# Conformer convolution layer: the token axis cut in two halves, norm and output projection of the first half placed beside the convolution of the second, output bias added early

## The reference, cut to what matters

```
x = x + conformer_conv(rms_norm(x, norm1_g[0]), ...)
x = x + hierarchical_moe(rms_norm(x, norm2_g[0]), ...)

def conformer_conv(h, w_in, b_in, dw, dw_b, ln_g, ln_b, w_out, b_out):
    u = h @ w_in + b_in
    a, g = jnp.split(u, 2, axis=-1)
    u = a * jax.nn.sigmoid(g)
    u = causal_depthwise_conv(u, dw, width=31) + dw_b     # per channel, over 31 tokens
    u = jax.nn.silu(layer_norm(u, ln_g, ln_b))            # mean and variance over the 1024 channels
    return u @ w_out + b_out
```

## Time and profile before

| what | value |
|---|---|
| median of three runs | 1702.82 us |
| the profiled execution | 1700.86 us, of which 1699.1 us are the span from the first to the last instruction |
| mean granted PE clock | 0.926 |
| busy: PE, DVE, ACT, POOL | 1408.8, 440.7, 328.0, 277.2 us |
| 16 DMA engines, mean rate | 278 GB/s |

### The profile page before, as it was taken

The page is one execution under the profiler, slowest core; times in us unless marked ns, Lnnn a source line. Parts: engine busy times, 40 slices in busy tenths (PEclk is TensorE's granted clock), DMA queues, the critical chain, the costliest instruction groups (busy, mean ns, idle before and its releaser), DMA issues.

```text
span 1699.1 us, 17050 instructions
## 1 busy us (share of the span) xinstructions
PE 1408.8 (83%) x6028; PEld 638.2 (38%) x6028; DVE 440.7 (26%) x858; ACT 328.0 (19%) x629; POOL 277.2 (16%) x381
## 2 busy tenths in 40 slices
PE   4996596898878788777599999996997888888784
PEld 2442144333223223232376676644332332233231
DVE  1699615111011111010333333325110110110112
ACT  2465311000000000000334434421010000000000
POOL 0688200211111111110000000000211111111110
PEclk9998697999999999898799999997998999999997
DMA  9122015789999999998600400315899999999994
GB/s 324 37 99 99 1 74 222 318 361 419 420 420 420 420 421 418 419 416 339 248 1 1 149 1 1 149 74 223 338 360 420 421 420 420 420 416 413 418 413 184
DMA packets 91249, 473.13 MB, mean 278 GB/s; under 512 B 19675, under 2 KB 19675, under 8 KB 40260
## 3 DMA queue, kind: packets, MB, share of 16 engines
q1 hardware_dynamic: 78500, 443.12, 64.3%
q0 software_dynamic: 10400, 16.82, 2.7%
q10 hardware_dynamic: 2304, 12.58, 1.9%
HBM read 466.43 MB, written 23.33 MB: 288 GB/s over the span
## 4 chain that ended last, share of the span: by engine, by line
PE 49%; DMA 33%; DVE 7%; POOL 4%; issue 3%; SPq 3%; ACT 1%; ACTq 0%; POOLq 0%; DVEq 0%
DMA ring<-in_moe_w 30%; PE banks L1273 19%; PE banks L1381 7%; PE banks L1221 5%; POOL scratch L515 4%; PE banks L1290 3%; PE banks L1414 3%; SPq L315 2%; PE banks L1170 2%; DVE banks L863 2%; PE banks L1473 1%; PE banks L1428 1%; PE banks L1455 1%; DMA area<-y_dram 1%; PE banks L1402 1%
## 5 line engine op out<-in xcount | busy, mean ns | idle before, releaser
L1273 PE MATMUL banks<-ring,scratch 128*64 128x512 f32 x1984 | 502.2, 657 | 143.8 <-DMA ring<-in_moe_w 131.3
L1273 PEld LDWEIGHTS banks<-ring,scratch 128*64 128x64 f32 x1984 | 157.9, 151 | 484.8 <-issue 484.8
L1006 DVE COPY scratch<-banks 128x256 f32<-128x256 f32 x65 | 27.6, 424 | 801.7 <-PE banks L1281 801.7
L1290 PE MATMUL banks<-ring,scratch 128*64 128x512 f32 x1008 | 231.8, 602 | 3.0 <-DVE scratch L1006 3.0
L680 ACT ACTIVATE scratch<-banks 64x512 f32<-64x512 f32 x65 | 38.2, 588 | 598.8 <-PE banks L1273 598.8
L533 POOL COPY at_out<-rows_out 128x1 int32 (+1 forms) x64 | 11.6, 181 | 705.2 <-ACT scratch L684 705.2
L515 POOL TENSOR_TENSOR scratch<-scratch 128x512 f32<-128x512 f32 x88 | 111.8, 1271 | 63.6 <-ACT scratch L652 51.6
L1381 PE MATMUL banks<-hT,ring 128*128 128x512 f32 x256 | 117.9, 604 | 0.8 <-DVE hT L820 0.8
L1170 PE MATMUL banks<-hT,ring 128*128 128x512 f32 x256 | 113.2, 603 | 0.7 <-issue 0.7
L1290 PEld LDWEIGHTS banks<-ring,scratch 128*64 128x64 f32 x1008 | 68.3, 137 | 118.7 <-issue 111.7
L1221 PE MATMUL banks<-ring,area 128*128 128x512 f32 x200 | 91.3, 609 | 10.6 <-ACT area L662 9.6
(11 more groups left out here) (205 smaller groups left out, 1144.6 us busy)
## 6 DMA issues: line engine op xcount, KB each, us to landing
ring<-in_moe_w SPq DMA_DIRECT2D x374, 1024.0 KB, 16.9
area<-in_moe_w SPq DMA_DIRECT2D x12, 1024.0 KB, 10.2
ring<-in_attn_w_qkv SPq DMA_DIRECT2D x12, 1024.0 KB, 14.6
ring<-in_conv_w_in SPq DMA_DIRECT2D x8, 1024.0 KB, 14.4
area<-y_dram ACTq DMA_DIRECT2D x8, 1024.0 KB, 7.9
ring<-in_conv_w_out SPq DMA_DIRECT2D x4, 1024.0 KB, 12.5
xn_dram<-area ACTq DMA_DIRECT2D x8, 512.0 KB, 2.7
hT<-in_moe_w SPq DMA_DIRECT2D x4, 1024.0 KB, 7.6
```

The costliest lines, as they stand in the source:

```text
L1273: last = mm(bank[2 + s][q * SLOTS:(q + 1) * SLOTS, :], xeT[s][:, j, h, :], w[:, c, :], start=c == 0, stop=c == NC - 1)
L1290: last = mm(bank[6 + s][q * SLOTS:(q + 1) * SLOTS, :], hidT[s][:, j, :], w2c[:, j, q * 512:(q + 1) * 512], start=j == 0, stop=j == 3)
```

## The change

The convolution now runs in 16 stages (q = 0 to 15): 8 channel tiles of tokens 0 to 255, then the same 8 of tokens 256 to 511. All instructions of a stage are 256 wide instead of 512. The gated values of all tiles stay in memory, since the second half's taps reach back 30 tokens. The mean and the reciprocal of the first half are written to PSUM, and its layer norm is placed on DVE and ACT after stages 9 and 10; the first two output groups follow on PE in stages 13 and 14, the next two around the last statistics. The output bias is no longer a matmul: it is loaded to all 128 partitions and POOL adds it to the residual before it starts on taps. The output groups use two PSUM banks in turn instead of four. The rest of the kernel keeps its work and order.

```diff
+TH = T // 2
+STAGES = 2 * NC
+LAG = 3
...
-        sq_ct = area1[:].rearrange("p (c t) -> p c t", c=NC)
+        sq_buf = [area1[:, 3072 + b * TH:3072 + (b + 1) * TH] for b in range(4)]
         uT = area2[:].rearrange("p (c t) -> p c t", c=NC)
         chan_rows = area3[0:TAPS + 5, 0:D]
-        b_out = area3[0:1, 3072:3072 + D]
+        b_wide = area2[:, 0:D]
         PAD = TAPS - 1
-        u_buf = [scratch[:, b * (T + PAD):(b + 1) * (T + PAD)] for b in range(2)]
-        base = 2 * (T + PAD)
-        sg = [scratch[:, base + b * T:base + (b + 1) * T] for b in range(2)]
-        tap = [scratch[:, base + (2 + b) * T:base + (3 + b) * T] for b in range(TAP_BUFS)]
-        pacc = [scratch[:, base + (5 + b) * T:base + (6 + b) * T] for b in range(2)]
-        sums = (bank[6], bank[7])
-        ln_mu = area3[:, 1024:1024 + T]
-        ln_r = area3[:, 1024 + T:1024 + 2 * T]
-        ln_t = area3[:, 1024 + 2 * T:1024 + 3 * T]
+        u_all = scratch[:, 0:NC * (T + PAD)].rearrange("p (c t) -> p c t", c=NC)
+        base = NC * (T + PAD)
+        sg = [scratch[:, base + b * TH:base + (b + 1) * TH] for b in range(2)]
+        tap = [scratch[:, base + (2 + b) * TH:base + (3 + b) * TH] for b in range(TAP_BUFS)]
+        pacc = [area3[:, 2560 + b * TH:2560 + (b + 1) * TH] for b in range(2)]
+        sums = (bank[6][:, 0:TH], bank[7][:, 0:TH])
+        glu_bank = (bank[0], bank[1])
+        ln_mu = area3[:, 1024:1024 + TH]
+        ln_r = area3[:, 1024 + TH:1024 + 2 * TH]
+        ln_t = area3[:, 1024 + 2 * TH:1024 + 3 * TH]
+        mu_wide = bank[6][:, TH:2 * TH]
+        r_wide = bank[7][:, TH:2 * TH]
...
+        def mix_order(l):
+
+            if l == 1:
+                return [(n, t) for n in range(2) for t in range(NT)]
+            return [(n, t) for hh in range(2) for n in range(2) for t in (2 * hh, 2 * hh + 1)]
...
-            return bank[k % 4 + 2 * l]
+            return bank[k % 4 + 2] if l else bank[k % 2 + 2]
...
-            sp.dma_start(b_out, conv_b_out).then_inc(params_loaded, 16)
+            sp.dma_start(b_wide, conv_b_out.to_broadcast([P, D])).then_inc(bias_loaded, 16)
...
-            moe_weights(0, [(glu_ready, 4)] * 2 + [(glu_ready, 8)] * 2 + [(mix_ready, 4), (mix_ready, 8)], first_qkv)
+            moe_weights(0, [(glu_ready, NC + 4)] * 2 + [(glu_ready, 2 * NC)] * 2 + [(mix_ready, 6), (mix_ready, 8)], first_qkv)
...
+            pool.wait_ge(bias_loaded, 16)
+            for t in range(NT):
+                pool.wait_ge(xn_done, t + 1)
+                g.tensor_tensor(x_res[:, t, :], x_res[:, t, :], b_wide, ALU.add).then_inc(bias_added, 1)
+
             k = 0
-            for ct in range(NC):
+            for q in range(STAGES):
                 for w in range(1, POOL_TAPS):
                     k += 1
-                    pool.wait_ge(tap_made, ct * POOL_TAPS + w + 1)
+                    pool.wait_ge(tap_made, q * POOL_TAPS + w + 1)
                     if w > 1:
                         pool.wait_ge(tap_added, k - 1)
-                    g.tensor_tensor(pacc[ct % 2], pacc[ct % 2], tap[(k - 1) % TAP_BUFS], ALU.add).then_inc(tap_added, 1)
...
+            def squares(q):
+                act.wait_ge(conv_done, q + 1)
+                if q >= 4:
+                    act.wait_ge(stats_done, q - 3)
+                a.activation(sq_buf[q % 4], conv_out(q), ACT.Square).then_inc(sq_done, 1)
+
+            def gate(q):
+                act.wait_ge(glu_ready, q + 1)
+                if q >= 2:
+                    act.wait_ge(u_done, q - 1)
+                a.activation(sg[q % 2], glu_bank[q % 2][:, TH:2 * TH], ACT.Sigmoid,
+                             bias=chan[:, q % NC, TAPS + 4:TAPS + 5]).then_inc(gate_done, 1)
...
+            for q in range(STAGES):
+                act.wait_ge(u_done, q + 1)
+                if q >= 2:
+                    act.wait_ge(conv_done, q - 1)
                 for w in range(POOL_TAPS):
-                    k = ct * (POOL_TAPS - 1) + w - 1
-                    dst = pacc[ct % 2] if w == 0 else tap[k % TAP_BUFS]
+                    k = q * (POOL_TAPS - 1) + w - 1
+                    dst = pacc[q % 2] if w == 0 else tap[k % TAP_BUFS]
                     if w >= 1 and k >= TAP_BUFS:
                         act.wait_ge(tap_added, k - TAP_BUFS + 1)
-                    a.activation(dst, u_buf[ct % 2][:, w:w + T], ACT.Copy, scale=chan[:, ct, w:w + 1]).then_inc(tap_made, 1)
-                    if w == POOL_TAPS // 2 and ct + 1 < NC:
-                        gate(ct + 1)
-                if ct >= 1:
-                    squares(ct - 1)
-            squares(NC - 1)
-            act.wait_ge(ln_var, 1)
-            a.activation(ln_r, ln_t, ACT.Sqrt, bias=eps[:]).then_inc(ln_std, 1)
-            for ct in range(NC):
-                act.wait_ge(ln_x, ct + 1)
-                a.activation(uT[:, ct, :], uT[:, ct, :], ACT.Silu, bias=chan[:, ct, TAPS + 2:TAPS + 3],
-                             scale=chan[:, ct, TAPS + 1:TAPS + 2]).then_inc(ln_done, 1)
+                    a.activation(dst, u_in(q, w), ACT.Copy, scale=chan[:, q % NC, w:w + 1]).then_inc(tap_made, 1)
+                    if w == POOL_TAPS // 2 and q + 1 < STAGES:
+                        gate(q + 1)
+                if q >= 1:
+                    squares(q - 1)
+                if q == NC + 1:
+                    ln_root(0)
+                if q == NC + 2:
+                    ln_silu(0)
+            squares(STAGES - 1)
+            ln_root(1)
+            ln_silu(1)
...
+            def ln_stats(hh):
+                dve.wait_ge(stats_ready, hh + 1)
+                link(v.tensor_scalar(ln_mu, bank[4][:, 0:TH], 1.0 / D, None, ALU.mult))
+                link(v.tensor_tensor(ln_t, ln_mu, ln_mu, ALU.mult))
+                link(v.scalar_tensor_tensor(ln_t, bank[5][:, 0:TH], 1.0 / D, ln_t, ALU.mult, ALU.subtract))
+                v.tensor_copy(mu_wide, ln_mu).then_inc(stats_taken, 1)
+                v.tensor_scalar(ln_t, ln_t, 0.0, None, ALU.max).then_inc(ln_var, 1)
+
+            def ln_apply(hh):
+                dve.wait_ge(stats_taken, hh + 1)
+                dve.wait_ge(ln_std, hh + 1)
+                link(v.reciprocal(r_wide, ln_r))
+                for ct in range(NC):
+                    xs = conv_out(NC * hh + ct)
+                    link(v.tensor_tensor(xs, xs, mu_wide, ALU.subtract))
+                    v.tensor_tensor(xs, xs, r_wide, ALU.mult).then_inc(ln_x, 1)
+
+            def add_group(l, k):
+                n, t = mix_order(l)[k]
+                dve.wait_ge(mix_ready, 8 * l + k + 1)
+                xs = x_res[:, t, n * 512:(n + 1) * 512]
+                ins = v.tensor_tensor(xs, xs, mix_bank(l, k)[:], ALU.add)
+                if n == 0:
+                    ins.then_inc(mix_taken, 1)
+                else:
+                    ins.then_inc(x_done, 1)
...
+                    if q == 0 and w >= TAPS - 2:
+                        dve.wait_ge(bias_added, NT)
...
+                if q == NC + 1:
+                    ln_stats(0)
+                if q == NC + 2:
+                    ln_apply(0)
+                if q == NC + 5:
+                    add_group(0, 0)
+                if q == NC + 6:
+                    add_group(0, 1)
+            ln_stats(1)
+            ln_apply(1)
...
+                if l == 0:
+                    for t in range(2):
+                        add_group(0, 2 + t)
+                        invert_rms(N_MOE[0], t)
+                    add_group(0, 4)
+                    take_hT(N_MOE[0], 0)
+                    add_group(0, 5)
+                    take_hT(N_MOE[0], 1)
+                    add_group(0, 6)
+                    invert_rms(N_MOE[0], 2)
+                    add_group(0, 7)
+                    invert_rms(N_MOE[0], 3)
+                    take_hT(N_MOE[0], 2)
+                    take_hT(N_MOE[0], 3)
...
+            def stats(q):
+                hh, ct = stage(q)
+                pe.wait_ge(sq_done, q + 1)
+                if hh == 1 and ct == 0:
+                    pe.wait_ge(stats_taken, 1)
+                mm(bank[4][:, 0:TH], ones[:], conv_out(q), start=ct == 0, stop=ct == NC - 1)
+                last = mm(bank[5][:, 0:TH], ones[:], sq_buf[q % 4], start=ct == 0, stop=ct == NC - 1)
+                last.then_inc(stats_ready if ct == NC - 1 else stats_done, 1)
+
+            def mix_group(l, k, n0, src, done, reuse):
+
+                n, t = mix_order(l)[k]
+                loaded(pe, n0 + n)
+                dst = mix_bank(l, k)
+                if reuse is not None:
+                    pe.wait_ge(*reuse)
+                for c in range(NC - 1 if k < ahead[l] else 0, NC):
+                    if done is not None:
+                        pe.wait_ge(done[0], done[1] + c + 1)
+                    last = mm(dst[:], src[:, c, t * P:(t + 1) * P], w_chunks(n0 + n)[:, c, :],
+                              start=c == 0, stop=c == NC - 1)
+                last.then_inc(mix_ready, 1)
...
+                if q >= LAG:
+                    stats(q - LAG)
```

(27 more changed lines are left out.)

167 lines of the change are left out of this document (71 added, 96 removed).

## The result

The changed kernel's median is 1707.17 us over 14 runs (1702.37 to 1711.65), that of the kernel before 1702.39 over 14 (1698.28 to 1707.11) in the same comparison. The ratio is 1.0029, 95% interval [1.0017, 1.0041]: 0.3% slower, which is measurable and lies within the 0.5% that I called no change. I had forecast 1703, within 0.5%. The profiled execution took 1703.22 us (span 1701.5) against 1700.86: a pair 2.4 apart, where the medians are 4.8 apart, because the one of the changed kernel is among the shortest of its 14 runs.

What follows compares the result with a forecast made beforehand. Bound: the experts' weight stream, so time ahead of the first expert moves everything; the convolution is a DVE, ACT, POOL loop. Convolution's end +37 and tail -37 sum to 0 against the profiled 1700.9, forecast median 1703, range 1690 to 1717.

Steps and rivals of the forecast that it cites:

- Earlier start: Start of the convolution: 256-wide projection records let the first taps start at 43.3 instead of 50.77, -7.4 us.
- Stage length: Convolution loop: 9.7 us per half-wide stage with POOL's add at 0.71 us, +24.5 us in all.
- The slower rival: POOL's adds in the convolution: larger fixed cost, add 0.81 us gives 1713, 0.89 gives 1725; chance 0.14.
- the faster one: Convolution loop: POOL's add proportional at 0.64 us and the loop closes up, 1696 or 1691; chance 0.22.
- Layer norm inside the loop: Stages 10 and 11: the first half's layer norm on DVE and ACT holds up the loop, +14.6 us.
- PE's order: Late convolution: groups 0 and 1 ahead of the projections of stages 14 and 15 delay POOL, +5.4 us.
- Tail: Behind the convolution: 256-wide layer norm, four groups without bias, and logits take 48.7 us against 85.7, -37.
- Routing and gather keep their 34.3 us.: Between the output groups and the experts: routing and first gather were to stay unchanged at 34.3 us.
- Experts: Expert stretch, paced by the weights' DMA: work unchanged, 508 us as before.
- Clock at the lower level through groups 0 and 1: PE late in the convolution: low clock ends the last projection 27 us later, 1730, half of it 1716; chance 0.07.
- Groups not hidden: Output groups 2 and 3 fall behind the layer norm, 13.8 us come back, 1717; chance 0.03.
- PE also keeps up: Late convolution, within the faster rival (chance 0.22): PE's groups delay nothing, another 5.4 us go, 1691.

Runs made afterwards that it cites:

- experiment 1: Kernel before at full width with only the early bias on POOL, bias matmuls gone: 1691.99 us, ratio 0.9933 to the kernel before.
- Experiment 4: Changed kernel without the first half's reciprocal, subtract, multiply and silu (output wrong): convolution ends 12.55 us earlier; median 1671.67 us not usable.
- Experiment 3: Changed kernel with output groups 0 and 1 behind the last projection on PE: 1702.22 us, ratio 0.9996 to the kernel before.
- Experiment 2: Changed kernel with the first half's apply and silu and groups 0 to 2 behind the last stage: 1709.18 us, ratio 1.0033 to the kernel before.

## Why the prediction came out right, step by step

- **Earlier start.** Predicted first tap 43.3, measured 41.90: -8.9 instead of -7.4. The small parameters, now without the bias's row, were there at 28.67, about 1 us earlier, which no term of mine had; experiment 1 has it too (first tap 49.56 for 50.80). The bias adds ran from 29.69 to 38.94, ahead of POOL's first product at 42.88, as predicted.
- **Stage length.** POOL's add: predicted 710 ns, measured 725. DVE's tap 484, measured 483. The stage: predicted 9.7, measured 9.75 (16 of 9.7 are 155.2, not the 155.4 of my sum, which changes nothing). The two widths give 1271 - 725 = 546 ns for 256 elements and a fixed part of 725 - 546 = 179 ns, where I took 150. The Trainium skill (GPSIMD Engine Reference, section 3.1) states about 2.6 cycles per element for a two-input add; at the 1.2 GHz that it reckons with, that is an estimated 555 ns for 256 elements, and the 546 of this trace agree within 2%. The slower rival needed 0.81, the faster one 0.64. Neither came.
- **Layer norm inside the loop.** Predicted: stage 10 takes 14.0, stage 11 20.0. Measured: 13.8 (141.39 to 155.17) and 20.0 (to 175.21). Experiment 4 takes 10.7 us of stage 11 out.
- **PE's order.** I had the projections of stages 14 and 15 end 48.1 and 62.8 us behind stage 9. Measured from 141.39 they end at 48.6 and 63.2. PE began slow and lost 2.8 us (2.5 predicted) in statistics and group 0. The four last stages took 44.9 us, predicted 44.2. Experiment 3 takes the wait out and shortens the convolution by 5.4 us from its first tap, as predicted.
- **End of the convolution.** 220.0 predicted, 220.10 measured. It is partly luck: the start was 1.4 us early and the stages 1.5 longer.
- **Tail.** -37 predicted; 85.6 us became 47.7, so -37.9. Group 4 started at 233.71 (233 predicted). The bias was priced at 1.05 a group; experiment 1 shows 1.1.
- **What the sum had as unchanged and wasn't.** "Routing and gather keep their 34.3 us." From the last group to the first expert it is now 37.4 instead of 34.4, all of it in the last two blocks of logits:

```profile
271.47 1.23 PE banks L1239 x8
272.69 2.69 PE banks L1347 x16
...
275.96 3.56 PE banks L1347 x16
279.52 0.58 PE banks L1348 x2
```

  They end 8.6 us after the last transposes begin; before, 5.5. This is the step that failed: I had looked at the clock in the old layer norm and in the middle, not at the end. Up to the first expert the sum is -8.9 + 46.0 - 37.9 + 3.0 = +2.2, and the profiled executions end 2.4 apart.
- **Experts.** They were to take the same time. From the first expert's transposes to DVE's first sum of their results it was 510.3 us before and 512.6 after, where the other kernels but number 4 had 509.3 to 513.6. That is +2.3, another term that I had put at nothing. It is not all scatter: the eight half-wide kernels average 512.1 and the five full-wide ones 510.2, for a reason that no run shows. But from that sum to the end of the span it is 883.6 us after and 885.8 before (884.5 and 886.7 on average), so these profiles give the 2 us back, and the +2.2 at the first expert is left. Whether the medians, 4.8 apart, got it back too is open.
- **The rivals.** Clock at the lower level through groups 0 and 1: it rose within group 0 (8.43 us, then 6.91). Groups not hidden: groups 0 to 2 lay inside the convolution or at its end. "PE also keeps up" is what experiment 3 forced, and it brought 5.6 us by the ratios, where I had 5.4.

So the balance closes near nothing, as forecast, and each of its large terms came within 2 us. The median still came out 4.2 us above the 1703: the logits' 3.0 is one part, and the other is not shown. Experiment 2 shows the half-wide loop with only the first half's statistics in it: it starts 7.7 us earlier than the full-width one of experiment 1 (first tap 41.82 against 49.56) and ends 22.7 us later (203.88 against 181.19). The overlap then saves 3.7 us at the last group. And the bias, which has nothing to do with halves, gives 11.5 in experiment 1. The forecast of no change was right as a sum of one good part and one bad one; I had not asked what either would do alone.

## What to carry to other kernels

When a loop is bound by one engine with small instructions, halving the tile costs its fixed part once more for each (here 1271 to 725 ns, and 0.14 us between two dependent adds), so look first for what can be had without halving: here the bias alone won 0.7%, and the full change lost 0.3%. A serial piece put inside such a loop cost its whole length here (10.7 us in its stage), and two groups queued ahead of two projections on another engine cost 5 more; no run tried the piece at another place in the loop. And PE's clock can fall where the sum has nothing: here that cost 3 us in two blocks of logits, and its cause stays open.
